# Spreading the mLSTM's running maximum: from a selecting product and a copy to a DMA from one row

## The reference, cut to what matters

```
b = cumsum(log_sigmoid(f_gate))
dmat = where(tril, b[t] - b[s] + li[s], -inf)
m_t = maximum(b + m, max_s dmat)
s = (q k^T) * exp(dmat - m_t)
num = w_inter * (C q) + s v ;  den = w_inter * (n . q) + sum_s s
h = num / maximum(abs(den), exp(-m_t))
```

## Time and profile before

| | |
|---|---|
| median of 3 runs | 2124.29 us (2123.27 to 2124.77) |
| the profiled execution: its own time | 2122.0 us |
| its span | 2120.2 us |
| mean granted TensorE clock | 0.965 of 2.4 GHz |
| PE busy | 1975.7 us (93%) |
| DVE, ACT, POOL busy | 1081.3, 758.0 and 71.3 us (51%, 36%, 3%) |
| chain that ended last | PE 85%, DVE 9%, ACT 3% |
| DMA | 266 MB, mean 126 GB/s |

### The profile page before, as it was taken

How to read it: one execution, slowest core, us unless ns; L and a number is a source line. 1 busy time by engine, 2 the same in 40 slices (tenths; PEclk the granted TensorE clock), 3 DMA queues, 4 the chain that set the end, 5 groups by cost and what they waited for, 6 DMA issues and landing times.

```text
span 2120.2 us, 34512 instructions
## 1 busy us (share of the span) xinstructions
PE 1975.7 (93%) x15200; PEld 1679.2 (79%) x15200; DVE 1081.3 (51%) x1653; ACT 758.0 (36%) x1060; POOL 71.3 (3%) x78
## 2 busy tenths in 40 slices
PE   5899999899989998899999989999998999899998
PEld 2667657678768776676899989998987777799998
DVE  2623563523324326555655465545756677456553
ACT  3423453311211224345433343333443433334332
POOL 0011000000000000010000000002001111000000
PEclk8899999999999999898999999999999999999999
DMA  8234202343434511211455545543441111144552
GB/s 321 83 127 179 71 21 100 115 164 139 161 133 144 179 61 50 70 40 41 159 179 181 177 149 182 184 172 131 158 149 61 42 42 42 61 168 151 182 178 79
DMA packets 37157, 266.22 MB, mean 126 GB/s; under 512 B 4112, under 2 KB 4112, under 8 KB 6672
## 3 DMA queue, kind: packets, MB, share of 16 engines
q1 hardware_dynamic: 36720, 260.87, 35.1%
q10 hardware_dynamic: 288, 3.15, 0.4%
HBM read 262.96 MB, written 1.05 MB: 125 GB/s over the span
## 4 chain that ended last, share of the span: by engine, by line
PE 85%; DVE 9%; ACT 3%; issue 1%; DMA 1%; SPq 0%; DVEq 0%; ACTq 0%
PE ps L568 19%; PE ps L569 19%; PE ps L570 19%; PE ps L2513 2%; PE ps L802 2%; PE ps L1142 2%; PE ps L642 2%; DVE W L548 2%; PE ps L1120 2%; PE ps L1346 1%; PE ps L574 1%; PE ps L1359 1%; PE ps L576 1%; PE ps L575 1%; PE ps L1131 1%
## 5 line engine op out<-in xcount | busy, mean ns | idle before, releaser
L548 DVE TENSOR_TENSOR W<-ring,W 128x2048 fp32r<-128x2048 f32 (+3 forms) x194 | 430.9, 2222 | 314.2 <-ACT W L539 314.0
L539 ACT ACTIVATE W<-ring 128x2048 fp32r<-128x2048 f32 (+3 forms) x194 | 359.0, 1852 | 188.1 <-PE ps L570 135.9
L568 PE MATMUL ps<-h_lat,W 128*128 128x256 f32 x1056 | 303.8, 288 | 11.9 <-DVE h_lat L680 7.7
L569 PE MATMUL ps<-h_lat,W 128*128 128x256 f32 x1056 | 301.3, 285 | 0.0
L570 PE MATMUL ps<-h_lat,W 128*128 128x256 f32 x1056 | 301.1, 285 | 0.0
L568 PEld LDWEIGHTS ps<-h_lat,W 128*128 128x128 f32 x1056 | 204.7, 194 | 14.4 <-issue 12.9
L569 PEld LDWEIGHTS ps<-h_lat,W 128*128 128x128 f32 x1056 | 205.4, 195 | 0.0
L570 PEld LDWEIGHTS ps<-h_lat,W 128*128 128x128 f32 x1056 | 205.2, 194 | 0.0
L767 ACT ACTIVATE work<-ps 128x256 f32<-128x256 f32 (+1 forms) x88 | 38.4, 437 | 392.6 <-PE ps L570 392.6
L785 DVE TENSOR_TENSOR work<-work,ps 128x256 f32<-128x256 f32 (+1 forms) x88 | 42.9, 487 | 238.1 <-ACT work L767 238.1
L568 PE MATMUL ps<-hidden_lat,W 128*128 128x256 f32 x528 | 152.4, 289 | 5.1 <-DVE hidden_lat L788 5.1
(11 more groups left out here) (343 smaller groups left out, 4032.1 us busy)
## 6 DMA issues: line engine op xcount, KB each, us to landing
ring<-w_up_dram SPq DMA_DIRECT2D x88, 1024.0 KB, 4.9
ring<-w_ada_dram SPq DMA_DIRECT2D x48, 1024.0 KB, 5.0
ring<-w_down_dram SPq DMA_DIRECT2D x43, 1024.0 KB, 4.9
ring<-w_rkv_dram SPq DMA_DIRECT2D x13, 1024.0 KB, 4.9
ring<-w_fm_dram SPq DMA_DIRECT2D x10, 1024.0 KB, 5.0
ring<-w_out_dram SPq DMA_DIRECT2D x8, 1024.0 KB, 4.9
ring<-w_gates_dram SPq DMA_DIRECT2D x8, 1024.0 KB, 5.0
ring<-w_qk_dram SPq DMA_DIRECT2D x6, 1024.0 KB, 4.9
```

The lines of the kernel that those rows point to most:

```text
L539: act.activation(slots[SLOT[s]][:, 0, 0:cols], ring[:, u % RING, 0:cols], ACT.Copy).then_inc(w_high, 1)
L548: dve.tensor_tensor(slots[SLOT[s]][:, 1, 0:cols], ring[:, u % RING, 0:cols], slots[SLOT[s]][:, 0, 0:cols], ALU.subtract).then_inc(w_low, 1)
L568: pe.matmul(o, slots[SLOT[s]][:, 0, at:at + cols], high, start=first, stop=False)
L569: pe.matmul(o, slots[SLOT[s]][:, 0, at:at + cols], low, start=False, stop=False)
```

## The change

Head 0 keeps the selecting product and the copy. For heads 1 to 3 the product and the copy are gone, and ACT issues a DMA for each direction, whose source is row h of `ml_neg`, on one partition, read 128 times, and whose destination is `nb[:, h % 2, d]`: 128 partitions of 2 KB. Those of head 1 are issued as soon as `ml_rows` has been counted, ahead of head 0's copies; those of heads 2 and 3 in step s = 1 of the head before, behind a wait for all `log_weights` of the head that last used the buffer. DVE's `log_weights` of heads 1 to 3 wait for the DMA (a semaphore for each buffer and direction).

```diff
 pe_qk_tile:
-            pe.wait_ge(ml_nbs, 2 * (4 * layer + (step + 1) // 4 + 1))
+            pe.wait_ge(ml_nbs, 2 * layer + 2)
 pe_mlstm, in step n = 4h + s:
-                    if s in (1, 2) and h < 3:
-                        running_max(h + 1, s - 1)
 act_mlstm:
+            def spread_running_max(h):
+
+                if h >= 2:
+                    act.wait_ge(ml_z, 8 * (4 * layer + h - 1))
+                for d in range(2):
+                    act.dma_start(nb[:, h % 2, d, :], ml_neg[h:h + 1, d, :].unsqueeze(1).broadcast_to([1, P, TA])).then_inc(ml_spread[h % 2][d], 16)
+            act.wait_ge(ml_rows, layer + 1)
+            spread_running_max(1)
...
-                    if s in (1, 2) and h < 3:
-                        take_running_max(h + 1, s - 1)
+                    if s == 1 and 1 <= h < 3:
+                        spread_running_max(h + 1)
 dve_mlstm, log_weights(n):
-                    dve.wait_ge(ml_nbs, 2 * (4 * layer + h) + d + 1)
+                    if h == 0:
+                        dve.wait_ge(ml_nbs, 2 * layer + d + 1)
+                    else:
+                        dve.wait_ge(ml_spread[h % 2][d], 16 * (layer + 1 if h == 2 else 2 * layer + (h + 1) // 2))
```

More of the change, by code:

```diff
@@ L1264, in build @@
         ml_cols_taken = sem("ml_cols_taken")
+        ml_spread = [[sem(f"ml_spread{b}{d}") for d in range(2)] for b in range(2)]
         ma = Area(2 * 2 * UNIT, W_N)
@@ L1323, in pe_mlstm, with running_max @@
             c0, _ = unit_tokens(layer, False)
[L1325 to L1329, removed]
+            def running_max(d):
+                n = 2 * layer + d
+                if d:
                     pe.wait_ge(ml_nbs, n)
@@ L1332, in running_max @@
                     pe.wait_ge(ml_cols_taken, layer + 1)
-                pe.matmul(ps[:, 4, 0:TA], K("sel")[0:4, h * P:(h + 1) * P], ml_neg[:, d, :], start=True, stop=True)\
-                    .then_inc(ml_nb, 1)
+                pe.matmul(ps[:, 4, 0:TA], K("sel")[0:4, 0:P], ml_neg[:, d, :], start=True, stop=True).then_inc(ml_nb, 1)
             def sums(h):
@@ L1348, in sums @@
                 mm.then_inc(ml_num, 1)
-            running_max(0, 0)
-            running_max(0, 1)
+            running_max(0)
+            running_max(1)
             for h in range(4):
@@ L1399, in act_mlstm @@
                 .then_inc(ml_enm, 1)
-            def take_running_max(h, d):
-                hh = 4 * layer + h
-                act.wait_ge(ml_nb, 2 * hh + d + 1)
+            def spread_running_max(h):
                 if h >= 2:
[L1405 to L1408, removed]
+                    act.wait_ge(ml_z, 8 * (4 * layer + h - 1))
[3 more added lines that the diff above has]
+            spread_running_max(1)
+            for d in range(2):
+                act.wait_ge(ml_nb, 2 * layer + d + 1)
+                act.activation(nb[:, 0, d, :], ps[:, 4, 0:TA], ACT.Copy).then_inc(ml_nbs, 1)
             for h in range(4):
```

## The result

The changed kernel takes 2142.95 us (median of 6 runs, 2133.13 to 2147.25), the kernel before beside it 2124.53 us (6 runs, 2121.19 to 2130.99). The ratio, taken over all executions, is 1.0069, with a 95% interval of 1.0039 to 1.0100 (the two medians alone would give 1.0087): slower, by more than the 0.2% that a measurement can tell. The profiled execution of the changed kernel took 2133.13 us with a span of 2131.3 us; before, 2122.0 and 2120.2 us. So the traces explain 11.1 us. The medians lie 18.4 us apart: four of the six executions took 2142.69 to 2147.25 us, at a mean granted clock of 0.955 to 0.959 against 0.962 in the other two (0.003 to 0.007 of 2140 us, an estimated 6 to 15 us), and no trace shows where they lose it.

The account below looks back on a forecast made before the run. PE's own work was taken to bound the steps. -12.6 us of products, +6.6 and +9.0 of waits and +6 of clock gave +9.0 us: 2131.0 on the profiled execution, 2133 predicted for the median, range 2109 to 2148 us.

Parts of the forecast that it names:

- forecast case: Whole kernel: slow one-partition copies make PE wait in layer 1; 2133 us, 2126 to 2148 for T 19 to 27; chance 0.43.
- 12 products and what hangs on them: Both layers' mLSTM: 12 selecting products of 1.05 us leave PE's stream, 6 for each layer; -12.6 us.
- layer 1: PE waits at head 2, head 3: Layer 1: T of 21.7 us exceeds the allowed 15.1 and 12.7 us, so PE stands 6.6 and 9.0 us.
- layer 1: clock: Layer 1, behind PE's gaps: a lowered granted clock costs 6.8 us at most, taken as 6 and counted once.
- T: Time from issuing a head's two DMAs (512 KB) until both have landed; taken as 21.7 us.
- the ends: Bounds on one partition's rate: 3.4 GB/s, making T 154 us, or 437 GB/s, as fast as the load.
- head 1 and all of layer 0 are hidden: Layer 1's head 1 and layer 0's heads 1 to 3: copies land before they are needed, so no PE wait.
- limits of 27 to 36 us: Layer 0: how long T may be without delaying PE: head 1 35.9, head 2 30.6, head 3 27.1 us.
- fourth rival: PE's saved 12.6 us turn into waits for weights: 2124 us; counted with the second rival, together chance 0.10.
- The prediction's own sign of being wrong: Wrong if a pair lands within 12 us, or if layer 0 too has gaps (then T is over 27 us).
- DVE's tail of 2.2 us: Layer 1, head 2: DVE's second `log_weights`, product 7 and query tile after the landing, 902.6 to 904.81 us.
- rows 10: Rows cited for the clock: PE nearly idle 962.7 to 970.7 us, then a L1120 pair took 2.00 us instead of 1.07.

Follow-up runs that it names:

- wide source: The changed kernel with its copies reading a constant tile on 128 partitions instead of one row on one partition: 2113.44 us, ratio 0.9930 to the kernel before.
- near rows: The changed kernel with each direction copied by four DMAs from constant rows on partitions 0, 1, 2, 3: 2138.59 us, beside 2125.62 us for the kernel before.
- staged copies: The changed kernel with rows 1 to 3 first copied to 32 partitions each, then spread from there: 2110.18 us, ratio 0.9923 to the kernel before.
- half the bytes: The kernel with the change in layer 1 alone, but copying only the 256 columns that layer 1 reads: 2116.90 us, ratio 0.9948 to the kernel before.
- unread copies: The kernel before, plus layer 0 copies of one row to 96 partitions that no result depends on: 2127.32 us, ratio 1.0005.
- four far rows: The changed kernel with each direction copied by four DMAs from constant rows on partitions 0, 4, 8, 12: 2112.26 us, beside 2125.62 us for the kernel before.

## Why the prediction was right, and where it was not

The forecast case came, slower, at 2143 us in a range of 2109 to 2148. Forecast were +9.0 us; measured are +11.1 between the traces and +18.4 between the medians. That the traces come so near is luck: the sum was right only as a sum. Set out with the wide source as the reference, whose products are gone and whose copies cost nothing:

| term | predicted | measured |
|---|---|---|
| 12 products and what hangs on them | -12.6 us | -9.6 (layer 0), -6.1 (layer 1) |
| layer 1: PE waits at head 2, head 3 | +6.6, +9.0 us | +2.38, +1.64 |
| layer 1: clock | +6 us | +6.1 (10.1 longer than the reference, less the waits) |
| layer 0: PE waits for weights | 0 | +3.29, +6.64 |
| layer 0: clock | 0 | +6.1 (16.1 longer, less the waits) |
| elsewhere | 0 | +0.6 (+1.5 ahead of layer 0, +3.1 between the layers, -4.0 behind layer 1) |
| sum | +9.0 us | +11.1 us |

Four errors nearly cancel: 11.6 us too much for the waits of layer 1 and 3.1 too little for the products, against 9.9 us of waits and 6.1 of clock in layer 0 that were put at nothing. The two clock terms are remainders, but PE's busy time for the same matmuls says the same (columns as in the earlier trace rows, one line for each layer). The changed kernel:

```profile
97.09:248.43 151.34, 140.72 (x860) 97.65 (x861) 48.12 (x116) 38.32 (x76) 17.75 (x32) 0.91 0.68 156
869.31:958.30 88.99, 83.98 (x462) 69.47 (x462) 39.09 (x113) 26.39 (x54) 9.32 (x16) 0.87 0.67 82
```

and the wide source:

```profile
98.11:233.37 135.26, 134.57 (x860) 94.87 (x862) 48.07 (x116) 38.29 (x76) 17.71 (x32) 0.96 0.46 167
856.17:935.03 78.86, 77.88 (x462) 63.98 (x462) 39.73 (x113) 26.40 (x54) 9.30 (x16) 0.94 0.23 84
```

That is 6.15 and 6.10 us more for as many matmuls. In layer 1 the low clock follows the gaps (0.50 from 918 to 925 us, above). In layer 0 an estimated half of it does; the rest lies in two stretches where PE had no gap (changed kernel):

```profile
130.00:135.00 5.00, 5.00 (x29) 3.01 (x29) 3.77 (x7) 3.50 (x7) 2.06 (x3) 0.66 0.10 11
...
180.00:190.00 10.00, 10.00 (x54) 6.74 (x53) 7.90 (x19) 2.28 (x6) 1.76 (x4) 0.83 0.90 27
```

They withhold 1.7 us each (5 x 0.34 and 10 x 0.17), where the wide source has 1.00 from 125 to 205 us. What lowered the clock there no run shows.

- **T was right.** Predicted 21.7 us, measured 20.7 (20.7 to 21.4 over the six pairs): the pair of head 2 in layer 1 was issued from 892.13 us, and the second row let DVE go at 912.88. The rate of one engine's share (27.3 GB/s) was the right choice between the ends, and the estimate from the Trainium skill (SBUF — State Buffer, section Door 1), 21.5 us, agrees too. The other formula of the Trainium skill (DMA: Bandwidth & Descriptors, section on the SWDGE path), an estimated 3.2 us for 512 KB, does not hold where one partition is the source; with the wide source a DMA of 256 KB took 2.5 us, close to the estimate of 2.6 us that the formula gives for it.
- **The step that failed: "head 1 and all of layer 0 are hidden".** The limits of 27 to 36 us counted only when DVE would want the row. The copies also hold up the weight loads, the ring holds 3 units, and the two loads that PE came to stand for left little room: before the change they were used 18.8 us (issued at 91.95 us, used at 110.71) and 8.4 us after their issue. The second one, before:

```profile
184.50 0.33 SPq L521 DMA_DIRECT2D ring<-w_ada_dram  x1
...
192.86 1.07 PE L802 MATMUL ps<-ring,const 128*32 128x256 f32 x16
```

The fourth rival spoke of waits for weights and was put aside because "the DMA share there leaves room". The share of before (0.32 from 140 to 175 us) did leave room, but a copy out of one partition fills it without moving much: 0.90 at 27 GB/s. Room is used by time, not by bytes, and some 20 us for each of three pairs could have been laid over the times at which weights are issued and used. The prediction's own sign of being wrong came with it: layer 0 has gaps, and not because T is over 27 us.
- **Layer 1's waits were over-sized, 15.6 us for 4.0.** Three causes are in the rows. First, the issue was placed behind the exponents of step 5; on the new time line that is 884.5 + 11.1 = 895.6 us, and the DMAs were issued at 892.13, 3.4 us earlier (below). Second, T was 1.0 us shorter: 6.6 - 3.4 - 1.0 = 2.2 us, and 2.38 were measured. DVE's tail of 2.2 us was right: released at 912.88, the tile at 915.09. Third, that gap and the half clock behind it held PE up, and so it came to `sums(2)` at 935.57 us instead of 917.5 + 11.1 = 928.6, 7.0 us later: of head 3's 9.0 us T takes off 1.0 and this 7.0, its issue came 0.6 us late, and 1.6 are left, as measured. That head 2's gap would be made up there was foreseen for the clock and not taken off head 3's 9.0 us.
- **The removed products** were worth more than their time in layer 0: 9.6 us for the 6.3 that six products are. See the last section.
- **The clock term had the right size from a misread row.** PE did not do "next to nothing" from 962.7 to 970.7 us: rows 10 are the chain of waits, which runs over ACT and DVE there, while PE's time line of the kernel before shows it at work until 968.03 us and standing for 2.67:

```profile
966.91 1.12 PE L1120 MATMUL ps<-work 64*128 64x512 f32 x2
970.70 1.11 PE L1131 MATMUL ps<-const,work 128*128 128x128 f32 x4 [2.67 <-DVE work L1193]
```

So a gap much shorter than 8 us was followed by half clock there. It need not be: in the trace of the changed kernel the same gap is followed by full clock,

```profile
985.77 0.66 PE L1131 MATMUL ps<-const,work 128*128 128x128 f32 x4 [2.68 <-DVE work L1193]
...
988.00:998.00 10.00, 10.00 (x55) 5.90 (x54) 5.80 (x17) 4.71 (x12) 0.00 (x0) 1.00 0.05 18
```

and with it goes the -4.0 us behind layer 1: 1173.0 us from ACT's square behind the layer to the end, where the nine other traces have 1176.3 to 1177.6. It is luck of this execution, not an effect of the change that any run shows; without it the traces would be 15 us apart.
- **The range** is a little off its own sum, which gives 2128 us at T = 19 and 2146 at T = 27 us instead of 2126 and 2148.

The issue, in the time line of ACT, after:

```profile
891.97 0.60 ACT L985 ACTIVATE work<-ps 128x512 f32<-128x512 f32 x1 [3.86 <-PE ps L570]
892.13 0.48 ACTq L1403 DMA_DIRECT2D work<-work  x1
...
892.63 0.62 ACTq L1403 DMA_DIRECT2D work<-work  x1
892.95 1.91 ACT L539 ACTIVATE W<-ring 128x2048 fp32r<-128x2048 f32 x1
894.75 0.72 ACT L1416 ACTIVATE work<-work 128x256 f32<-128x256 f32 x2
```

In the written order the two L1403 stand behind L539 and the exponents L1416. They are issued at 892.13 us, while ACT is still at L985, and the exponents run at 894.75.

And what followed on DVE, after:

```profile
907.77 0.55 DVE L1505 TENSOR_SCALAR work<-work 128x256 f32<-128x256 f32 x1
912.88 0.35 DVE L1505 TENSOR_SCALAR work<-work 128x256 f32<-128x256 f32 x1 [4.57 <-DMA work<-work]
```

The first direction's row was there in time; the second, behind it on the same way out, held DVE for 4.57 us. Of these PE saw 2.38, because it had other work until 912.71.

## What to carry to other kernels

A DMA that reads one SBUF partition ran at about 27 GB/s here, whether it wrote 32, 96 or 128 partitions: cost it by bytes over that rate, and for that long expect weight loads on the other queue, and their issue, to be held up. Read how late a load may be from the distance between its issue and its use, not from the mean DMA share. Where a row must go to all partitions, spread it first to 32 and then out from those: the same products are removed, and the kernel gains 0.8% instead of losing 0.7%. Where only half of the row is read, sending that half was enough in layer 1.

## What was not expected of the hardware

- **A DMA's issue passes work that stands ahead of it on its engine.** ACT issued the copies 2.6 us before the exponents written ahead of them (892.13 and 894.75 us, rows above). They went 0.16 us after L985's wait for PE had ended: waits held them up, the arithmetic in front of them did not. So the written order, in which the prediction placed them, is not the order in which a DMA starts.
- **An issue has no fixed price.** On ACT it took 0.47 to 0.63 us with the wide source, where SP's had 0.33; with the DMA engines full, 3.4 us on ACT (near rows), 5.92 us on ACT (layer 1 alone) and 8.00 us on SP.
- **The clock of layer 0 rose when small products left, with no gap in sight.** From 125 to 150 us PE has work all the time in these kernels; columns as in the earlier trace rows. Before:

```profile
125.00:150.00 25.00, 25.00 (x156) 16.82 (x156) 11.02 (x27) 6.75 (x14) 3.79 (x6) 0.88 0.38 132
```

with the staged copies:

```profile
125.00:150.00 25.00, 25.00 (x163) 17.94 (x156) 10.28 (x26) 5.98 (x13) 3.72 (x6) 1.00 0.56 189
```

and with half the bytes in layer 1, where layer 0 keeps its products, further on:

```profile
175.00:205.00 30.00, 30.00 (x156) 19.50 (x155) 14.30 (x32) 7.77 (x16) 3.08 (x7) 0.89 0.39 136
```

Each kernel that kept the products in layer 0 shows such a stretch there in its trace, at 0.85 to 0.89 (before, layer 1 alone, half the bytes, unread copies); the three that had neither the products nor slow copies (wide source, four far rows, staged) show 1.00 from 125 to 205 us. A granted clock of 0.88 over 25 us is 25 x 0.12 = 3.0 us, close to the 3.3 us that layer 0 gained beyond its six products. That the products cause it is what these traces suggest, but no run took it apart, and the products cannot be all of it: the changed kernel, which has none there, falls to 0.66 from 130 to 135 us without a gap (above), and the change in layer 0 alone to 0.93 from 150 to 175 us.
